# First RMS norm of a hybrid two-layer trunk taken from token rows, with table preparation placed behind the first two projection blocks

## The reference, cut to what matters

```python
h = jnp.concatenate([meta, x], axis=1)            # 528 tokens x 1024 channels
for layer in range(DEPTH):                        # DEPTH = 2
    u = h * lax.rsqrt(jnp.mean(h*h, axis=-1, keepdims=True) + EPS) * norm_g[layer]
    (gq, gk, gv, ga, g_gate, s_in, s_gate, aq, ak, av, a_gate, m_gate) = _split_in(u @ w_in[layer])
    y_gla = ...   # gated linear attention; its decay gate comes from ga @ w_a2
    y_s5  = ...   # S5: complex poles a_re, a_im and a step exp(log_dt), from which matrices are built
    y_att = ...   # sliding-window attention with a relative-position bias from rel_bias
    h = h + (merge of the three) @ w_out[layer]
return _rmsnorm(h, final_norm_g)[:, N_META:]
```

## Time and profile before

| what | value |
|---|---|
| median of 3 runs | 1890.58 us (1886.93 to 1893.35) |
| the profiled execution, from first to last instruction | 1894.7 us |
| PE busy | 1747.2 us, 92% of the span |
| DVE / ACT / POOL busy | 49% / 37% / 42% |
| mean granted TensorE clock | 0.958 of full speed |
| start of the first projection | 38.22 us |

### The profile page before, as it was taken

The page is one execution under the profiler, slowest core; times in us unless marked ns, Lnnn a source line. Parts: engine busy times, 40 slices in busy tenths (PEclk is TensorE's granted clock), DMA queues, the critical chain, the costliest instruction groups (busy, mean ns, idle before and its releaser), DMA issues.

```text
span 1894.7 us, 31165 instructions
## 1 busy us (share of the span) xinstructions
PE 1747.2 (92%) x12985; PEld 1538.7 (81%) x12985; DVE 927.3 (49%) x1471; ACT 701.2 (37%) x1332; POOL 788.6 (42%) x490
## 2 busy tenths in 40 slices
PE   5967899999998999988997999999999898999997
PEld 4967798999887889987897987777788676788885
DVE  7985134333438992374453222533334598624223
ACT  3453442444543113332233543334455322224322
POOL 1655575333232223332343685653332332344442
PEclk8988999999999999998898999999999998999999
DMA  8543244322375653535342433542223956433432
GB/s 146 149 108 105 72 115 118 85 67 72 92 153 131 158 146 107 112 82 149 87 124 55 133 90 90 113 118 78 67 75 101 169 156 155 124 100 92 143 104 85
DMA packets 363539, 209.56 MB, mean 111 GB/s; under 512 B 75524, under 2 KB 350136, under 8 KB 360840
## 3 DMA queue, kind: packets, MB, share of 16 engines
q1 hardware_dynamic: 350600, 187.92, 38.7%
q10 hardware_dynamic: 12800, 19.66, 3.5%
HBM read 170.34 MB, written 36.67 MB: 109 GB/s over the span
## 4 chain that ended last, share of the span: by engine, by line
PE 68%; DVE 10%; POOL 7%; DMA 5%; ACT 5%; issue 3%; SPq 2%; ACTq 1%; DVEq 0%; POOLq 0%
PE ring L844 52%; DMA sb_w_raw<-in_w_in 4%; POOL sb_w_lo L686 3%; PE ring L803 3%; DVE sb_s_prod L1631 2%; PE ring L825 2%; PE aux L1115 1%; SPq L580 1%; PE aux L1224 1%; PE aux L1160 1%; PE aux L1136 1%; DMA s_matrices<-sb_s_phase 1%; DVE sb_s_rot L2136 1%; DVE sb_s_rot L1631 1%; PE aux L1163 1%
## 5 line engine op out<-in xcount | busy, mean ns | idle before, releaser
L686 POOL TENSOR_TENSOR sb_w_lo<-sb_w_raw,sb_w_hi 128x1024 fp32r<-128x1024 f32 x246 | 609.0, 2477 | 1026.3 <-ACT sb_w_hi L1275 1023.9
L1275 ACT ACTIVATE sb_w_hi<-sb_w_raw 128x1024 fp32r<-128x1024 f32 x246 | 260.0, 1057 | 602.7 <-DMA sb_w_raw<-in_w_in 398.7
L844 PE MATMUL ring<-sb_u_hi,sb_w_hi 128*128 128x264 f32 (+1 forms) x2112 | 368.5, 329 | 24.6 <-DVE sb_tmp_dve L1711 14.6
L844 PEld LDWEIGHTS ring<-sb_u_hi,sb_w_hi 128*128 128x128 f32 x2112 | 314.3, 203 | 63.3 <-DVE sb_tmp_dve L1711 16.5
L844 PE MATMUL ring<-sb_u_lo,sb_w_hi 128*128 128x264 f32 (+1 forms) x2112 | 340.8, 312 | 0.0
L844 PE MATMUL ring<-sb_u_hi,sb_w_lo 128*128 128x264 f32 (+1 forms) x2112 | 334.6, 309 | 0.0
L844 PEld LDWEIGHTS ring<-sb_u_lo,sb_w_hi 128*128 128x128 f32 x2112 | 300.6, 192 | 22.0
L844 PEld LDWEIGHTS ring<-sb_u_hi,sb_w_lo 128*128 128x128 f32 x2112 | 294.1, 188 | 21.0
L1307 ACT ACTIVATE sb_tmp_act<-ring 128x528 f32<-128x528 f32 (+1 forms) x112 | 67.3, 601 | 138.6 <-PE ring L844 135.8
L1746 DVE SCALAR_TENSOR_TENSOR sb_tmp_dve<-sb_tmp_act,ring 128x528 f32<-128x528 f32 (+1 forms) x32 | 22.3, 696 | 142.0 <-PE ring L844 130.0
L1551 ACT ACTIVATE sb_att_scores<-sb_att_scores,sb_att_neg_max 128x208 f32<-128x208 f32 x128 | 58.5, 458 | 82.7 <-DVE sb_att_neg_max L1929 82.7
(11 more groups left out here) (333 smaller groups left out, 2455.7 us busy)
## 6 DMA issues: line engine op xcount, KB each, us to landing
sb_w_raw<-in_w_in SPq DMA_DIRECT2D x166, 512.0 KB, 4.1
sb_s_loaded<-s_matrices ACTq DMA_DIRECT2D x16, 1040.0 KB
s_matrices<-sb_s_phase SPq DMA_DIRECT2D x16, 528.0 KB, 3.1
sb_w_raw<-in_w_gla_out SPq DMA_DIRECT2D x16, 512.0 KB, 3.5
sb_w_raw<-in_w_attn_out SPq DMA_DIRECT2D x16, 512.0 KB, 3.5
sb_w_raw<-in_s_w_glu SPq DMA_DIRECT2D x16, 512.0 KB, 3.5
sb_w_raw<-in_w_s_out SPq DMA_DIRECT2D x16, 512.0 KB, 3.5
sb_w_raw<-in_w_out SPq DMA_DIRECT2D x16, 512.0 KB, 3.5
```

Source lines behind the costliest of these rows:

```text
L686: pool.tensor_tensor(WL[:, w], WR[:, w], WH[:, w].bitcast(F32), ALU.subtract).then_inc(lo_ready, 1)
L844: last = pe.matmul(RING[:, 2 * r + hf, 0:c1 - c0], w[:, n % SLOTS, kt, :], moving(b[0], xx[:, kt], c0, c1), start=(term == 0 and kt == 0), ...
L1275: act.activation(WH[:, w], WR[:, w], ACT.Copy).then_inc(hi_ready, 1)
```

## The change

The sums of squares are taken from x as it arrives, with tokens on the partitions: ACT squares each 128x1024 tile and accumulates over the row (L1416 of the changed kernel), giving a 128x5 table. DVE turns it into inverse RMS values and multiplies the identity by them, giving five diagonal matrices; PE multiplies these by ones (L870), which spreads the scales over all partitions in PSUM. DVE reads them there when it makes u. The squares of `H`, the sixteen matmuls of sums and the 128x528 square root and reciprocal of layer 0 are gone; layer 1 keeps its way.

The loads of the S5 poles go from SP's queue to ACT's. The loads of the bias inputs go behind those of blocks 0 to 2. The widening of the S5 rows goes between the copies of x. The bias matmul goes behind the projection of the first two blocks on PE, and its copy on DVE, the pole columns and the whole S5 preparation go behind u.

```diff
-                    sp.dma_start(S5R[r0:r0 + PAIRS], aa[ly].rearrange("(q g) n -> q (g n)", g=2)
...
+                    act.dma_start(S5R[r0:r0 + PAIRS], aa[ly].rearrange("(q g) n -> q (g n)", g=2)
...
-    head = [("norm", 0)] + [("gate", h) for h in range(4)]
+    head = [(ly, ("norm", 0))] + [(-1, ("bias", 0))] * (ly == 0) + [(ly, ("gate", h)) for h in range(4)]
...
+            def scale_rows():
+
+                h = aux_take(0, ("norm", 0))
+                pe.wait_ge(xdiag_ready, 1)
+                cols = [(0, 0, N_META)] + [(t + 1, N_META + P * t, N_META + P * t + P) for t in range(4)]
+                for t, c0, c1 in cols:
+                    rows = N_META if t == 0 else P
+                    for a, b in ((c0, min(c1, HALF)), (max(c0, HALF), c1)):
+                        if a < b:
+                            hf = a // HALF
+                            last = pe.matmul(AX_[:, 2 * h + hf, a - HALF * hf:b - HALF * hf], ONES[0:rows, :],
+                                             XD[0:rows, t, a - c0:b - c0], start=True, stop=True)
+                last.then_inc(aux_full[h], 1)
...
                 project_two_as_made(ly, (("ga", 0), ("gk", 0)), UH, UL, ulo_ready, KT * ly)
-
+                if ly == 0:
+                    bias_table()
...
-            hi_part(0)
-            hi_part(1)
+            def row_squares():
+
+                act.wait_ge(xsq_clear, 1)
+                for t in range(5):
+                    act.wait_ge(x_loaded[(t + 4) % 5], 16)
+                    x, n = (XIN[:, t - 1], P) if t else (MIN[:], N_META)
+                    act.activation(XQ[0:n, t], x, ACT.Square, accum_out=XSS[0:n, t:t + 1])
+                act.drain().then_inc(xsq_ready, 1)
+                act.wait_ge(xvar_ready, 1)
+                act.activation(XRS[:], XSS[:], ACT.Sqrt).then_inc(xstd_ready, 1)
+                hi_part(0)
+                hi_part(1)
...
+            def row_scales():
+
+                dve.wait_ge(xsq_ready, 1)
+                dve.tensor_scalar(XSS[:], XSS[:], 1.0 / D_MODEL, EPS, ALU.mult, ALU.add).then_inc(xvar_ready, 1)
+                dve.wait_ge(xstd_ready, 1)
+                link(dve.reciprocal(XRS[:], XRS[:]))
+                for t in range(5):
+                    last = dve.tensor_scalar(XD[:, t], ID[:], XRS[:, t:t + 1], None, ALU.mult)
+                last.then_inc(xdiag_ready, 1)
...
-            prepare = s5_prepare()
-            aux_read(dve, -1, ("s5p", 0))
-            next(prepare)
-            next(prepare)
             for ly in range(DEPTH):
-                inverse_rms(ly, ("norm", 0))
+                if ly:
+                    inverse_rms(ly, ("norm", 0))
+                    scale = two(TD[:, 0])
+                else:
+                    row_scales()
+                    h_norm = aux_result(dve, ly, ("norm", 0))
+                    scale = halves(aslot(h_norm))
...
+                if ly == 0:
+                    dve.engine_nop().then_inc(aux_free[h_norm], 1)
+                    prepare = s5_prepare()
+                    pole_columns()
+                    bias_table()
+                    aux_read(dve, -1, ("s5p", 0))
                 gla_gates(ly)
```

More of the change, by code:

```diff
@@ L858, in filler @@
                     project(ly, b, UH, UL)
-            def norm_sum(k0, name, ly):
-                h = aux_take(ly, name)
-                for kt in range(KT):
-                    pe.wait_ge(sq_ready, k0 + kt + 1)
-                    for hf, c0, c1 in column_parts(0):
-                        last = pe.matmul(AX_[:, 2 * h + hf, 0:c1 - c0], ONES[:], TA[:, kt % 2, c0:c1],
-                                         start=(kt == 0), stop=(kt == KT - 1))
-                    last.then_inc(sq_used if kt < KT - 1 else aux_full[h], 1)
+            def scale_rows():
[10 more added lines that the diff above has]
+                last.then_inc(aux_full[h], 1)
             def norm_sum_added(ly):
@@ L874, in norm_sum_added @@
                     if kt:
[L875 removed]
+                        pe.wait_ge(sq_ready, KT)
                     else:
@@ L941, in tokens_out, with bias_table @@
                 last.then_inc(aux_full[h], 1)
+            def bias_table():
+                pe.wait_ge(rel_loaded, 32)
+                h = aux_take(-1, ("bias", 0))
+                for c0, c1 in ((0, 512), (512, REL_COLS)):
+                    last = pe.matmul(AX_[0:ATT_HEADS, 2 * h + c0 // 512, 0:c1 - c0], TA[0:REL_BUCKETS, 0, 0:ATT_HEADS],
+                                     TD[0:REL_BUCKETS, :, :].rearrange("p a b -> p (a b)")[:, c0:c1],
+                                     start=True, stop=True)
+                last.then_inc(aux_full[h], 1)
             pe.wait_ge(id_ready, 2)
@@ L960, in _ @@
             pe.transpose(AX_[:, 2 * h, 0:52], PRS[:], ID[0:52, 0:52]).then_inc(aux_full[h], 1)
-            pe.wait_ge(rel_loaded, 32)
-            h = aux_take(-1, ("bias", 0))
-            for c0, c1 in ((0, 512), (512, REL_COLS)):
-                last = pe.matmul(AX_[0:ATT_HEADS, 2 * h + c0 // 512, 0:c1 - c0], TA[0:REL_BUCKETS, 0, 0:ATT_HEADS],
-                                 TD[0:REL_BUCKETS, :, :].rearrange("p a b -> p (a b)")[:, c0:c1],
-                                 start=True, stop=True)
-            last.then_inc(aux_full[h], 1)
             h = aux_take(-1, ("s5p", 0))
@@ L1416, in _ @@
                 else:
[L1417 to L1424 removed]
+                    row_squares()
+                if ly:
+                    act.wait_ge(var_ready, 1)
+                    act.activation(TD[:, 1], TD[:, 0], ACT.Sqrt).then_inc(std_ready, 1)
                 for kt in range(KT):
@@ L1474, in _ @@
                                            ).then_inc(aux_free[h], 1)
+                    if ly == 0 and b == ("gk", 0):
+                        aux_read(act, -1, ("bias", 0))
                     if kind == "gv" and j in GATE_AT[ly]:
@@ L1651, in _ @@
                 last.then_inc(aux_free[h], 1)
+                if i == 4:
+                    dve.wait_ge(s5_rows, 16 * (2 * DEPTH + 1))
+                    dve.tensor_copy(LDB[:], LDR[:].unsqueeze(2).broadcast_to([DEPTH * PAIRS, 2, S5_STATE]))
+                    for g in range(2):
+                        dve.tensor_copy(S5RX[:, S5_STATE * g:S5_STATE * g + S5_STATE],
+                                        S5R[:, S5_STATE * (1 - g):S5_STATE * (1 - g) + S5_STATE])
+                        last = dve.tensor_copy(LDBX[:, g], LDR[:, 1 - g:2 - g].broadcast_to([DEPTH * PAIRS, S5_STATE]))
+                    last.then_inc(dt_wide, 1)
             for i in range(9):
@@ L1679, in _, with bias_table, pole_columns @@
-            last.then_inc(aux_free[h], 1)
+            def bias_table():
+                h = aux_result(dve, -1, ("bias", 0))
+                dve.tensor_copy(BROW[:, 0:512], AX_[0:ATT_HEADS, 2 * h, 0:512])
+                link(dve.tensor_copy(BROW[:, 512:REL_COLS], AX_[0:ATT_HEADS, 2 * h + 1, 0:REL_COLS - 512]))
+                dve.drain().then_inc(bias_rows_sb, 1)
+                dve.engine_nop().then_inc(aux_free[h], 1)
+            def pole_columns():
+                h = aux_result(dve, -1, ("s5p", 0))
+                for x in range(2):
+                    for ly in range(DEPTH):
+                        dve.tensor_copy(S5P[:, ly, 0:2].rearrange("p r (a x) -> p r a x", x=2)[:, :, :, x],
+                                        AX_[:, 2 * h, P * x:P * x + P]
+                                        .rearrange("p (l r a x) -> p l r a x", l=DEPTH, r=2, x=2)[:, ly, :, :, x])
+                    last = dve.tensor_copy(S5P[:, :, 2].rearrange("p l (a x) -> p l a x", x=2)[:, :, :, x],
+                                           AX_[:, 2 * h + 1, DEPTH * PAIRS * x:DEPTH * PAIRS * (x + 1)]
+                                           .rearrange("p (l a x) -> p l a x", l=DEPTH, x=2)[:, :, :, x])
+                last.then_inc(aux_free[h], 1)
```

70 lines of the change are left out of this document (24 added, 46 removed).

## The result

The kernel after takes 1900.34 us against 1892.38 us before (medians of 20 runs each), a ratio of 1.0036 with a 95% interval from 1.0021 to 1.0051. The ratio makes that 6.8 us slower (4 to 9.7; the two medians lie 8.0 us apart), where I forecast 4.1 us. The interval of the ratio does not reach 1, and the middle of it lies just above the 0.3% that the prediction took as the bound of what can be told. Against the median of before that the prediction started from (1890.6 of three runs) the 1900.34 us lie 0.3 us above the end of its range; against the 20 runs the +6.8 us lie inside. I had given 0.31 to a kernel slower by more than 0.3% and 0.60 to one that can't be told from no change; it came out just in the first of the two.

The account below looks back on a forecast made before the run. Bound taken as PE's row of matmul blocks (chain 68% PE). 17.7 us gained at the start, then +3.9 at `gk` 3 from late weights, +4.1 with ACT's work: 1894.7 us against a median of 1890.6, range 1885.5 to 1900.0.

Parts of the forecast that it names:

- Start of the projection: PE's first projection of two blocks: to start at 20.5 us, 17.7 us earlier than before.
- diagonals meet POOL: DVE's last diagonals held by POOL's low parts: projection 3.7 us later, +7.8 us, 1898.4 us; chance 0.18.
- Issue of the write: SP's issue of the bias-table write, behind the projection: at 37.1 us, 11.6 us later than before.
- Length of the write: Bias-table write on SP's queue: 25.8 us from issue to landing, as before, so landing at 62.9.
- Block 3's landing: Weight block 3, queued behind the bias-table write on SP's queue: its data there at 65.0 us.
- Everything lands in order in the queue: SP's queue: transfers go through one behind another; evidence was block 4's 11 us behind the spill.
- `gk` 2 behind an idle PE: PE's block `gk` 2 after 19 us of idleness: takes 7.12 us and not 5.82, ending at 73.8.
- S5 preparation at nothing: DVE's S5 preparation, ending at about 91 us with PE: costed at nothing, covered by the DMA wait.
- The price without the cover: Rival, weights pass the bias table: DVE's preparation becomes the bound, 0.2 to 4.4 us faster; chance 0.21.
- The note on POOL: POOL's phases wait for the preparation's end, some 15 us ahead of their old distance to PE; costed at nothing.
- The rival that the start's gain is kept: Queue and DVE's preparation both shorter: up to 16 us at `gk` 1 come through; half, 8 us, gives 1882.6; chance 0.08.

Follow-up runs that it names:

- the diagonals first: Kernel after, with POOL's first low part of a weight block waiting until the five diagonals are made: ratio 1.0033 to the kernel before.
- the early kernel in pieces with the same edit: Kernel after with bias table ahead of the projection, its write in four pieces, POOL's first low part waiting for the diagonals: ratio 0.9935 to before.
- the write twice: Kernel after with a second bias-table write of the same size, to another buffer, right behind the first: ratio 1.0165 to the kernel before.
- the write behind block 4: Kernel after with the whole bias-table write on SP's queue, issued behind block 4: ratio 0.9990 to the kernel before.
- the kernel with less of it: Kernel after with the S5 preparation's second exponential replaced by 1 + x, 3.5 us less for DVE: ratio 1.0038 to the kernel before.
- the write in pieces: Kernel after with the bias-table write in four pieces of 16 rows, one behind each of blocks 4 to 7: ratio 0.9999 to the kernel before.
- the four kernels with the table early and the preparation behind the projection: Kernel after, bias table ahead of projection: alone 0.9968; write in pieces 0.9962; second exponential 1 + x 0.9946; pieces and POOL waiting for diagonals 0.9935.

## Why the prediction was right, and where it was off

The sign and the mechanism were right: the projection starts much earlier, the write of the bias table moves behind it and so becomes later, the weights queue behind the write, and PE stands idle ahead of `gk` 2. By its own steps:

- *Start of the projection*, forecast 20.5, measured 23.24: the first mis-sized term. The diagonals were to end at 15.6 and ended at 17.73, since POOL's first low part held one of them; and the spreading matmuls with their handover took 3.2 us instead of 1.7. Of these 3.6 us the forecast had 0.9 in hand, as PE was to wait for the low parts anyway. With the diagonals first, the start was at 20.86, and the spreading with its handover took 2.6 us. That shorter spreading goes with the clock and not with the edit: the granted clock was still 1.00 from 15 to 16 us there and 0.50 in the kernel after, and in the early kernel in pieces with the same edit, where it was 0.50 from 15 us on too, the spreading matmuls took 3.01 us again.
- *The rival "diagonals meet POOL"* thus came true by half. Its first step happened (a diagonal stands for a whole low part); its second, that the next diagonal meets the second low part, did not, as the diagonal that was held was the last one. I had given it 0.18 as a whole and 24.2 as the start. It should have been a term of the sum with its own size; its +7.8 us are nearer to the measured +6.8 than the forecast's +4.1.
- *Issue of the write*, forecast 37.1, measured 39.36: 2.3 us of the 2.7 came through, the projection being 0.3 us shorter (14.05) than before.
- *Length of the write*: 26.4 us for a forecast 25.8. *Block 3's landing*: forecast 65.0, measured 67.36 (the start of its high part), late by the same 2.3 us. *Everything lands in order in the queue*: shown by the write twice and by the write behind block 4. That the spill's issue would hold SP for 19.27 us I had not foreseen; block 4 came at 74.25 all the same, 6.9 us behind block 3 where I had put 7. That this term came out so well is luck.
- *`gk` 2 behind an idle PE*: it took 82.38 - 68.97 - 5.82 = 7.59 us for a forecast 7.12; the granted clock is 0.50 in the window of 56 to 60 us ahead of it. Together: the forecast's 3.9 + 2.3 + 0.5 = 6.7 us for a measured 6.6 at the end of `gk` 3, and 6.55 at the second matrix.
- *S5 preparation at nothing*: right, shown by the kernel with less of it. *The price without the cover*: right in direction; with the write in pieces DVE was the bound. The note on POOL, that its phases wait for the end of the preparation, was only a clause without a price; in the kernel with pieces PE waited 6.80 us for it, and then still 2.20 us for DVE.
- *The rival that the start's gain is kept* did not come true for this kernel. It came near in the four kernels with the table early and the preparation behind the projection: there 6 to 12 us came through, with DVE, POOL and the weights close behind one another as the next bounds.

## What to carry to other kernels

When work is moved behind another piece, look for what it feeds: here a copy of 1 us feeds a transfer of 26 us, on the queue that brings the weights. Such a transfer wants to be issued where its queue has nothing to bring for as long as it takes (0.9968 here), or at least behind the loads that are needed next (0.9990) or in pieces between them (0.9999). And a single point deep in the program, read from each trace, tells 2 us where timed runs that scatter by 15 us do not.

## What the runs showed of the hardware

- *Two queues share the DMA engines by rows, it seems, not by bytes.* The write is 1024 rows of 2400 B, block 4 is 1024 rows of 512 B. On different queues both ended together (the write 29.8 us behind its issue, at 68.4, the block at 68.7) at 120 to 126 GB/s from 48 to 64 us, where the write alone has 101: 101 x (2400 + 512) / 2400 = 122.5. One row of each in turn would give just this. It is worked out, and no run varied the size of the rows. The Trainium skill, "DMA: Bandwidth & Descriptors", section "Queues, rings and completion order", says that each engine goes round the queues that have work, a packet at a time; the trace agrees that neither queue is ahead of the other, and shows that this is no protection: the load took 32 us instead of 10.
- *An issue behind a long queue holds the engine that issues.* The spill's issue, 0.58 us before the change, took 19.27 us behind the write and a block. That the queue was full is inferred. Here it seems to have cost nothing, since block 4 came 6.9 us behind block 3, as I had put it without this wait.
- *The write is slow, whole or in pieces*: 2.4 MB in 25.8 to 26.6 us wherever it was first in SP's queue, at a DMA share of 0.93, so the engines are busy with it. The pieces were no faster: two of them issued at 24.03 ran at some 100 GB/s. Why it is slow stays open: its source lies on 16 partitions and its rows have 2400 B, and no run varied either.
